# A decoder-step kernel on one core: eight more tokens moved from the dense expert pass to gathered rows, two query heads projected for both token groups at once, and three reorderings before them

## What is computed

```
h = rmsnorm(x);  q,k,v = split(h @ w_in)             # 16 heads (dilated windows) + 16 heads (window 128)
x = x + concat(rms(attn_A), rms(attn_B)) @ w_out
x = x + cross_attn(rmsnorm(x), 256 memory tokens)    # 4 heads of 128, w_cq, w_co
h = rmsnorm(x)
q = (h @ w_pq).reshape(tokens, 8 heads, 2 x 128)     # product keys: 128 x 128 = 16384 experts
s1, s2 = q1 @ sub_k1.T, q2 @ sub_k2.T;  top 16 of each, top 16 of their 256 sums -> expert ids, gates
y = sum over 8 heads x 16 experts of  gate * gelu(h . U[expert]) * V[expert]
x = x + y;  final rmsnorm
```

## Time and profile before

| | |
|---|---|
| median of three runs | 2310.1 us |
| the profiled execution | 2311.11 us, its span 2309.2 us |
| PE, PE weight load | busy 2207.9 us (96%), 2015.7 us (87%) |
| DVE, ACT, POOL | 1179.1 us (51%), 301.2 us (13%), 386.3 us (17%) |
| mean granted TensorE clock | 0.984 |
| moved | 843.21 MB, mean 365 GB/s |

### The profile page before, as it was taken

The page is one execution under the profiler, slowest core; times in us unless marked ns, Lnnn a source line. Parts: engine busy times, 40 slices in busy tenths (PEclk is TensorE's granted clock), DMA queues, the critical chain, the costliest instruction groups (busy, mean ns, idle before and its releaser), DMA issues.

```text
span 2309.2 us, 35404 instructions
## 1 busy us (share of the span) xinstructions
PE 2207.9 (96%) x14282; PEld 2015.7 (87%) x14282; DVE 1179.1 (51%) x2095; ACT 301.2 (13%) x926; POOL 386.3 (17%) x414
## 2 busy tenths in 40 slices
PE   7999998789889879999999999999999999999998
PEld 5677776577589868999999999899999999999998
DVE  3200003833566647767777544599744444444422
ACT  2000001722221012011111110144200000000000
POOL 0100000022302011232212221133311111111100
PEclk9999999999999989999999999999999999999999
DMA  7999982289959898999999999999999999999974
GB/s 280 405 413 381 385 316 81 80 333 357 398 201 396 345 383 315 407 398 422 422 421 420 420 420 420 372 372 376 402 422 421 422 422 421 422 422 422 421 315 155
DMA packets 117787, 843.21 MB, mean 365 GB/s; under 512 B 14432, under 2 KB 16608, under 8 KB 30656
## 3 DMA queue, kind: packets, MB, share of 16 engines
q1 hardware_dynamic: 62752, 485.30, 52.4%
q0 software_dynamic: 54128, 354.58, 37.7%
q10 hardware_dynamic: 816, 2.11, 0.2%
HBM read 834.25 MB, written 74.78 MB: 394 GB/s over the span
## 4 chain that ended last, share of the span: by engine, by line
PE 64%; DMA 23%; DVE 8%; issue 2%; ACT 1%; POOL 1%; SPq 0%; DVEq 0%; POOLq 0%; ACTq 0%
PE low L1414 39%; PE big L1414 24%; DMA BIG<-expert_u,VB 20%; DVE BIG L1240 4%; DMA WR<-wall 1%; DMA BIG<-kaT 1%; ACT BIG L630 1%; DMA BIG<-expert_v,VB 1%; DMA BIG<-memT 0%; DMA BIG<-va 0%; DVE CST L968 0%; POOL BIG L525 0%; DVE BIG L846 0%; PE low L1538 0%; DVE HT L883 0%
## 5 line engine op out<-in xcount | busy, mean ns | idle before, releaser
L1414 PE MATMUL low<-HT,WR 128*128 128x176 f32 (+3 forms) x6336 | 1081.9, 333 | 8.4 <-DMA WR<-wall 7.0
L1414 PEld LDWEIGHTS low<-HT,WR 128*128 128x128 f32 x6336 | 984.2, 191 | 98.2 <-issue 9.7
L1414 PE MATMUL big<-BIG,WR 128*128 (+3 forms) x2888 | 450.7, 312 | 11.3 <-DVE XT L891 7.1
L1253 DVE SCALAR_TENSOR_TENSOR XT<-BIG,VB,XT 128x2048 f32<-128x2048 f32 x128 | 300.9, 2351 | 302.7 <-DMA BIG<-expert_v,VB 302.4
L1414 PE MATMUL low<-BIG,WR 128*128 (+3 forms) x2616 | 434.8, 321 | 12.6 <-DMA WR<-wall 10.3
L1414 PEld LDWEIGHTS big<-BIG,WR 128*128 128x128 f32 x2888 | 419.3, 193 | 30.1 <-issue 18.5
L1240 DVE SCALAR_TENSOR_TENSOR BIG<-BIG 128x2048 f32<-128x2048 f32 x144 | 329.5, 2291 | 210.8 <-DMA BIG<-expert_u,VB 209.7
L1414 PEld LDWEIGHTS low<-BIG,WR 128*128 128x128 f32 x2616 | 411.0, 192 | 17.8 <-issue 10.5
L539 POOL DMA_INDIRECT BIG<-expert_u,VB x144 | 161.5, 1122 | 683.8 <-DVE BIG L1240 609.5
L545 POOL DMA_INDIRECT BIG<-expert_v,VB x144 | 161.5, 1122 | 558.2 <-DVE XT L1253 477.3
L914 DVE TENSOR_SCALAR BIG<-low 128x320 f32 x32 | 15.7, 492 | 264.0 <-PE low L1414 264.0
(11 more groups left out here) (230 smaller groups left out, 1124.0 us busy)
## 6 DMA issues: line engine op xcount, KB each, us to landing
WR<-uT SPq DMA_DIRECT2D x128, 1024.0 KB
WR<-expert_v SPq DMA_DIRECT2D x128, 1024.0 KB
WR<-wall SPq DMA_DIRECT2D x122, 1024.0 KB
BIG<-va POOLq DMA_DIRECT2D x48, 512.0 KB, 11.0
BIG<-kaT POOLq DMA_DIRECT2D x64, 384.0 KB, 11.0
BIG<-kmT SPq DMA_DIRECT2D x2, 2048.0 KB, 12.9
BIG<-vm SPq DMA_DIRECT2D x8, 512.0 KB, 13.4
XT<-xT SPq DMA_DIRECT2D x1, 2560.0 KB, 21.9
```

What stands on the lines that cost most here:

```text
L1253: nc.vector.scalar_tensor_tensor(out=x_tok, in0=rows_of(row), scalar=weight, in1=x_tok, op0=ALU.mult, op1=ALU.add).then_inc(s_vsum, 1)
L1414: return nc.tensor.matmul(out, lhsT, rhs, start=start, stop=stop, skip_group_check=True)
```

## The change

Seven edits. (1) 8 more tokens are gathered: `FEWER = 8` tokens x 16 half-heads fill 128 partitions, 8 more slots (`ROWS = 152`), and `DENSE` is 168. (2) Maps are 42, spread over U chunks 80 to 121, one a chunk, in three banks instead of four. (3) Rows are in another order: 58 rows from `ROWS_AHEAD` to `ROWS_BEFORE = 108` with two parts of the choice to five rows, then 5 rows to 4 chunks. (4) `pq` tiles 12 to 15 (heads 6 and 7) are made for all 320 tokens at once; tile 11 moves behind `co`, so cross-attention keeps one filler tile of four. (5) Memory keys and values are loaded at other places, half of the second values early into free space. (6) Prompt attention has a third probability buffer from pair 5 on, and the maximum goes out before the normalising. (7) In sample attention the adds of tiles made with the scores (and two cross queries) go before the softmax; `co` tiles of the first group rotate over three banks from tile 6 on.

```diff
-FEW = 16
+FEW, FEWER = 16, 8
+ALONE = FEW + FEWER
 REST = NT - P
-DENSE = REST - FEW
+DENSE = REST - ALONE
-EXPS, TAIL = 64, 80
-TURN = 92
-MAP_LO, MAP_HI = 100, 124
+EXPS, TAIL = 56, 64
+TURN = 72
+MAP_LO, MAP_HI = 80, 122
+E2_AT = 98
-ROWS = SLOTS + FEW
+ROWS = SLOTS + FEW + FEWER
+V_FEW = (*range(SLOTS, SLOTS + FEW), *range(40), *range(SLOTS + FEW, ROWS), *range(40, SLOTS))
 ROWS_AHEAD = 50
-ROWS_BEFORE = 141
+ROWS_WEIGH = 98
+ROWS_BEFORE = 108
-    return 2 if c % 3 == 0 else 1
+    return 2 if c % 4 == 0 else 1
-FEW_OUT = 96
+FEW_OUT, FEWER_OUT = 32, 96
...
-         + tiles_of("cq", 1, 0, 4) + tiles_of("pq", 0, 10, 14) + tiles_of("co", 1, 0, 16) + tiles_of("pq", 0, 14, 16)
-         + tiles_of("pq", 1, 0, 16))
+         + tiles_of("cq", 1, 0, 4) + tiles_of("pq", 0, 10, 11) + tiles_of("co", 1, 0, 16) + tiles_of("pq", 0, 11, 12)
+         + tiles_of("pq", 1, 12, 16) + tiles_of("pq", 1, 0, 12))
+BOTH_ORDER = (*range(12, 16), *range(12))
...
-                if before == POS["out", 1, 15]:
+                if before == POS["cq", 1, 0]:
                     sp.wait_ge(s_used, FREED["out", 1, 15])
                     mem_keys(0)
-                    mem_values(0)
+                    mem_values(0, 0, 4)
+                    sp.wait_ge(s_sc, 3)
+                    sp.wait_ge(s_idx, 3)
+                    mem_values(1, 0, 2)
                 if before == POS["pq", 0, 10]:
                     sp.wait_ge(s_cS, V_REQ[0] + 1)
                     mem_keys(1)
-                if before == POS["pq", 0, 12]:
+                if before == POS["co", 1, 0]:
                     sp.wait_ge(s_cV, 1)
-                    mem_values(1)
+                    mem_values(1, 2, 4)
...
             for h in range(PH):
-                act.dma_start(chosen[FEW * h:FEW * (h + 1), :, SLOTS:ROWS], few_src[:, :, h * PK:(h + 1) * PK]).then_inc(s_few, 16)
+                act.dma_start(chosen[FEW * h:FEW * (h + 1), :, SLOTS:SLOTS + FEW], few_src[:, :, h * PK:(h + 1) * PK]).then_inc(s_few, 16)
+                for half in range(2):
+                    to, k = half * 64 + h * FEWER, h * PK + half * FEWER
+                    act.dma_start(chosen[to:to + FEWER, :, SLOTS + FEW:ROWS], fewer_src[:, :, k:k + FEWER]).then_inc(s_few, 16)
...
-                    if p >= 2:
-                        dve.wait_ge(s_T, 2 * p - 2)
+                    if pair_in_buffer(p) >= 0:
+                        dve.wait_ge(s_T, 2 * pair_in_buffer(p) + 2)
...
-                if n + 1 < REQ:
-                    softmax_s(n + 1)
-                for f in (*with_scores, *with_turn):
+                for f in with_scores:
                     add_to_stream(FIRST_TILE, CROSS, f)
...
+                if n + 1 < REQ:
+                    softmax_s(n + 1)
+                for f in with_turn:
+                    add_to_stream(FIRST_TILE, CROSS, f)
...
+                if row[0] == SLOTS:
+                    dve.wait_ge(s_udot, SLOTS)
+                    nc.vector.tensor_copy(h_tok.rearrange("p (k h t) -> p k h t", k=KT, h=P // FEWER), HT_by[:, :, P + FEW:P + ALONE].unsqueeze(2).broadcast_to([P, KT, P // FEWER, FEWER])).then_inc(s_rep, 1)
...
-                if n % 3 == 0 and later:
+                if (n - ROWS_AHEAD) % 5 in (0, 2) and later:
                     choose_part(*later.pop(0))
...
+            def turn_fewer(part):
+
+                pe.wait_ge(s_rep, 2)
+                if part:
+                    pe.wait_ge(s_fewer_h, part)
+                for k in range(4):
+                    at = (4 * part + k) * P
+                    ins = nc.tensor.transpose(bank[7][:, k * P:(k + 1) * P], h_tok[:, at:at + P], ident)
+                ins.then_inc(s_fewer_t, 1)
```

More of the change, by code:

```diff
@@ L293, in build, with probs_p @@
         x_tok = XT_by[:, :, 0:P]
+        def probs_p(p):
+            buffer = p % 2 if p < OF_THREE else (2, 1, 0)[(p - OF_THREE) % 3]
+            if buffer == 2:
+                return q_pairs[0][:, :, 0:256], q_pairs[1][:, :, 0:P]
+            return probs_two[:, buffer, :, 0:256], probs_two[:, buffer, :, 256:384]
         def rows_of(x):
@@ L305, in tile_out @@
             if g == FIRST_TILE:
-                at = f % 2 if stage == "pq" else 5 + f % 2
+                at = f % 2 if stage == "pq" else (5, 6, 0)[(f - 6) % 3] if stage == "co" and f >= 6 else 5 + f % 2
             else:
                 at = (2, 3, 7)[f % 3] if stage in ("out", "co") else 2 + f % 2
-            return bank[at][:, 0:WIDTH[g]]
+            return bank[at][:, 0:NT if stage == "pq" and g == THE_REST and f >= 12 else WIDTH[g]]
         def sum_out(g, u):
@@ L810, in _ @@
                 nc.scalar.activation(late[:, 0:m], u[:, 0:m], ACT.Gelu).then_inc(s_dev, 1)
+                if E2_AT <= c < E2_AT + 4:
+                    part = c - E2_AT
+                    act.wait_ge(s_fewer_t, part + 1)
+                    nc.scalar.activation(h_tok[:, part * 512:(part + 1) * 512], bank[7], ACT.Copy).then_inc(s_fewer_h, 1)
                 if c == DOTS_DONE:
@@ L1537, in turn_p @@
                     for b in range(3):
-                        ins = nc.tensor.transpose(bank[s][:, b * P:(b + 1) * P], probs_p[:, p % 2, s, b * P:(b + 1) * P], ident)
+                        wide, narrow = probs_p(p)
+                        ins = nc.tensor.transpose(bank[s][:, b * P:(b + 1) * P], wide[:, s, b * P:(b + 1) * P] if b < 2 else narrow[:, s], ident)
                     ins.then_inc(s_T, 1)
@@ L1622, in wide @@
                 at = arrived(stage, g, f)
+                cols = slice(0, NT) if stage == "pq" and g == THE_REST and f >= 12 else COLS[g]
                 for k in range(KT):
-                    if f == 0:
+                    if f == (12 if stage == "pq" and g == THE_REST else 0):
                         pe.wait_ge(s_gh[g], normed + k + 1)
-                    h = h_own[k] if stage == "cq" and g == FIRST_TILE else x[:, k * NT:(k + 1) * NT][:, COLS[g]]
+                    h = h_own[k] if stage == "cq" and g == FIRST_TILE else x[:, k * NT:(k + 1) * NT][:, cols]
                     ins = mm(tile_out(stage, g, f), WR[:, at + k * P:at + (k + 1) * P], h, start=(k == 0), stop=(k == KT - 1))
@@ L1645, in co_tile @@
                 else:
[L1646 removed]
+                    pe.wait_ge(s_xadd[g], KT + f - (1 if g == FIRST_TILE and f < 8 else 2))
+                if g == FIRST_TILE and f == 8:
+                    pe.wait_ge(s_smax, 2 * REQ)
                 at = arrived("co", g, f) + f % 4 * 512
@@ L1906, in dense_v @@
                         pe.wait_ge(s_dev, NCH - UB + k // 2 + 1)
-                    ins = mm(v_all[k][:, FEW:REST], WR[:, slot_of(r) * D + k * P:slot_of(r) * D + (k + 1) * P], coefs, start=(first and k % 2 == 0), stop=last)
+                    ins = mm(v_all[k][:, ALONE:REST], WR[:, slot_of(r) * D + k * P:slot_of(r) * D + (k + 1) * P], coefs, start=(first and k % 2 == 0), stop=last)
                     if last:
```

170 lines of the change are left out of this document (101 added, 69 removed).

## The result

The changed kernel takes 2320.74 us (2320.22 to 2321.47, 4 runs) where the kernel before takes 2310.07 (2305.84 to 2310.73, 4 runs): a ratio of 1.005, 95% interval 1.0033 to 1.0068. It is slower by half a per cent, clear of the noise; 2291 was forecast, 2270 to 2312 was the range. The profiled execution took 2321.47 us, its span is 2319.7.

A forecast was written before the change was run, and what follows sets the result against it. PE was taken to bound U and the maps, full transfers most of V; the change would make transfers bound the maps. Stages before the dense passes -20 us, dense passes +1, so 2291 us, range 2270 to 2312.

The forecast's parts named there:

- Equal shares in V: V pass: chunk and row streams move equal bytes, so while rows last a chunk starts every 4.98 us.
- U before the maps: Dense pass over U up to the first map: 380 us, bounds 365 and 390, PE-bound.
- End: After the last row, now no longer hidden: 19 us where there were 16, bounds 16 and 22.
- Maps: Map stretch, 48 chunks: 268 us, bounds 256 and 297, transfers the bound with 105 of 2.49 us.
- The pass over V to its last row: V pass: 136 rows left, about 646 us to the last row, bounds 636 and 652; PE ends at some 626.
- The credit of "some 12": V pass: some 12 us taken off 637 us for what both rings hold.
- The even ledger: Dense passes: 16 added row transfers cost 40 us, matched by 40 us less idle transfer time; 1313 against 1312 us.
- Before the dense passes: Stages ahead of the dense passes: -20 us together, from prompt, sample and cross-attention and the third bank of `co`.
- Prompt attention: Prompt stage: third buffer and earlier maximum give -4 us, bounds -5 and 0.
- Cross-attention: Cross stage: -14 for weight wait and earlier second values, +10 for moved fillers, +1.5 for group sum; net -3, bounds -12 and +8.
- the second rival: Two of three losses: sample stage -4 not -12, cross-attention +6 not -3, dense chunks at 4.98 (+10); 2307 us, chance 0.24.
- That rival: Map stretch becomes the bound at 6.18 us a chunk: 297 us, +29, giving 2320 us; chance 0.15.

The follow-up runs named there:

- The run with 120 rows: Changed kernel with ROWS_BEFORE 120 instead of 108, and the eight tokens' values made ready earlier to match: 2288.59 us, 0.9904 of the kernel before.
- the run of the early edits alone: Kernel before plus only the third probability buffer, the moved softmaxes and the third bank of `co`: 2298.79 us, 0.9953.
- without the dense edit: Changed kernel with the dense passes of before (16 gathered tokens, 176 columns, 44 maps from chunk 100): 2292.14 us, 0.9929 of the kernel before.
- rows 24 us earlier: Changed kernel with ROWS_BEFORE 124 and the sum over the few tokens' rows made 16 chunks earlier: 2305.88 us, against 2307.87 with the later sum.

## Why the prediction was wrong

*What bounds each stretch* of the kernel before was read rightly: it is bound by chunks, with bytes to spare at the end, and rows added have to be taken up by idle time of the transfers. Equal shares in V were right: 4.97 us a chunk beside rows, with 168 columns as with 176. The Trainium skill, DMA: Bandwidth & Descriptors, "Queues, rings and completion order", says round robin between the queues that have work, and these 4.97 us, at 422 GB/s twice the 2.49 of 1 MB, agree with it.

*Where the error lies.* The profiled span was forecast at 2290 and is 2319.7: 20 us of the 30 are in the dense passes (+21 for +1), nearly all of them in one term, the pass over V; 10 are in the stages before them.

*U before the maps*: 380 forecast, 378.9 measured. *End*: 19 and 21.2. *Maps*: 268 and 263.9, but with fewer rows in it than the sum had: they move 398 GB/s, 100 transfers of 1 MB, where 105 were counted and called the bound; TensorE is busy 255.9 of the 263.9 us. The rows came back slowly behind the pause (348 GB/s from 1365.5 to 1400, 6 us lost), and the step to V cost the 4.39 us wait above, the "about 5" of the prediction.

*The pass over V to its last row* is the step that failed: 646 forecast, 669.1 measured. Three terms were wrong. 136 rows were to be left, 140 were: 12 had been started at V's first chunk, not 16; four rows by 2.49 are 10 us. The credit of "some 12" for what both rings hold was 5 at most: the pass moves 417 GB/s over its 669.1 us, that is 266 transfers for the 268 rows and chunks that it uses. That is 7 us. And its slow end, priced at full rate, costs 6: behind TensorE's last chunk the last rows move 337 GB/s from 2275 to 2296 us and nothing behind that. TensorE's own end of the pass came at 646 us where "some 626" was forecast; 10 of these it stood at its first V chunk, in three waits like the 4.12 us row above, for ScalarE's last gelus, which stood behind VectorE's late products (L1426). The rows lost nothing by that (423 GB/s from 1629.4 to 1645).

*The even ledger hid a hole.* "40 us more to move, 40 us less idle" was the second reason given for an even result, and it is wrong. By the windows' GB/s against 421, idle time from the dense start to the end of V was 66 us before (3 in U, 22 in the maps, 41 in V) and is 51 after (31, 14 and 6): 15 us less, not 40. The moved bytes grew by 31 us, since three of the rows were done ahead of the dense start. The prediction's own parts had most of the hole: its 380 us before the maps hold 346 us of transfers, and it worked out that the rows would be done after 63 chunks and 17 chunks would go alone, 78 us. It took that as cheap for TensorE and never set it against the idle time won. From 1320 to 1380 us that is (420 - 241) / 420 of 60 us = 26 us, and it came due at the end of V, because the added rows had made the rows the later of the two there. The run with 120 rows shows both ends of it: +2 us where the pause was, -32 at the end. So the V term tells why the forecast missed, and the pause tells why the change costs time at all. That 120 rows land at 2289, near the forecast of 2291, confirms nothing: it is another kernel.

*Before the dense passes* -20 was forecast, -10.3 came. Prompt attention gave 3.5 of 4 (its end at 460.5 for 464.0). At the last stop for sample attention the two together are worth 14.2 us in the run of the early edits alone (656.1 for 670.3; 16 forecast) and 11.2 in the changed kernel (659.05). There the 3.5 us stalls of the earlier trace rows are gone, and between the places where they were stands this row, one of five in turn that wait for values of the cache, 2.7 us together:

```profile
564.10 0.64 PE L1470 MATMUL big<-BIG 128*32 128x256 f32 x8 [0.65 <-DMA BIG<-va]
```

So cache transfers, named in the rival, take part of the gain, as far as this stretch shows; the rest of the difference was not traced. *Cross-attention*: TensorE after, at the first scores, the first filler and the first `co` tile:

```profile
806.84 1.93 PE L1470 MATMUL big<-BIG 128*32 128x256 f32 x32 [1.01 <-DVE BIG L1124]
816.62 5.95 PE L1470 MATMUL low<-HT,WR 128*128 128x128 f32 x32 [7.85 <-DMA WR<-wall]
...
839.58 0.69 PE L1744 MATMUL big<-CST,BIG 128*128 128x128 f32 x2 [3.71 <-DMA BIG<-vm]
844.12 3.64 PE L1470 MATMUL big<-BIG 128*32 128x512 f32 x16 [3.85 <-issue]
...
852.96 2.84 PE L1470 MATMUL low<-BIG,WR 128*128 128x192 f32 x16 [2.46 <-issue]
```

The 6.99 us wait is gone and `co` (the output projection of cross-attention) starts at 852.96 instead of 874.25; the wait for the second values fell from 8.89 to 3.85 us (the wait just before it grew from 1.68 to 3.71). But the first filler waits 7.85 us for weights, which are queued behind the memory's loads, as feared in the second rival, and the tile takes 5.95 us where such a tile takes 3.74 elsewhere, at a granted clock of 0.50 in its first 2.3 us. From the first `co` tile to the dense start it takes 133.6 us where it took 122.7, 10.9 more, as forecast (11.5). Net +1 in the profile instead of -3. That the edits still gain 6.6 us without the dense edit comes later: three more rows are done at the dense start, and the wait for the first map is gone.

*The rivals.* The maps did not become the bound: 5.50 us a chunk, not 5.98 or more. That rival gave almost the measured time, 2320, by a mechanism that did not happen; the match is luck. Of the second, its first two parts came about half and its third not. Its sum was also wrong: its parts are 8, 9 and 10 us, so two of them give 2308 to 2310, not "2302 to 2312". The chance of slower stood at 0.16 and nearly all of it on the wrong mechanism; what happened, rows late at the end of V, was priced in the sum and had no rival of its own.

## What to carry to other kernels

When two streams share full transfers and one engine consumes both, write down for each pass when each stream ends, and look for any stretch in which one stream has nothing to ask for. In this kernel the lost bytes were paid only where that stream was the last to end, and then in full. A change that moves work from matmuls to transfers needs its split points (here the number of rows ahead of the maps) set anew; 108, 120 and 124 rows gave 2321, 2289 and 2308 us. Relief for the stream that ends first was worth nothing clear of the noise: rows 24 us earlier gave 2 us, 16 transfers less gave none. And when forecast and ledger are two ways to the same number, set the idle time of the parts into the ledger.

## What was not expected of the hardware

Between a chunk and a row each every 4.97 us and a chunk alone every 4.77 or 4.56 us there is a third state: once TensorE has stood still for a few us and its ring is full, it goes at its own pace beside rows for about a dozen chunks (kernel before, 4.77 us from the rows at 2149.98 above to its last row; changed kernel, eleven chunks at 4.56 from 1807.3 us). An estimate from these times fits: it gains 0.41 us with each chunk on a stream that brings one in 4.97, so one chunk in store lasts for twelve. That it is the store, no run shows by itself.

The end of the changed kernel looks as if row transfers alone could not fill the transfers: 285 GB/s from 2275 to 2300 us. Taken apart it is not so:

```profile
2275.00:2281.00 6.00, 0.44 (x4) 0.18 (x2) 5.75 (x3) 0.00 (x0) 5.39 (x3) 0.80 0.79 272
2281.00:2290.00 9.00, 0.00 (x0) 0.00 (x0) 6.93 (x4) 0.00 (x0) 8.09 (x4) 0.50 1.01 395
2290.00:2296.20 6.20, 0.00 (x0) 0.00 (x0) 5.48 (x4) 0.00 (x0) 1.53 (x1) 0.50 0.84 313
```

First VectorE works without a pause through rows that have landed, at 2.4 us each, and holds their places in the ring; then rows alone move 395 GB/s; then the last ones drain, and behind 2296.2 nothing moves. TensorE has nothing to do in this time, and its granted clock stands at 0.50, the lower of its two levels, from 2281 us on.
